# An attention-heavy two-block fp32 model on one core: the order of work around its attentions

## The reference, cut to what matters

```
# dilated mixer: 3 groups (window, dilation), 16 heads of 64, one softmax over the groups' shares
o = sum_g wts_g * softmax(q_g k_g^T / 8, masked) v_g ;  x = x + o @ w_o
# cross attention, per layer of the second block, 4 heads of 256
q = rmsnorm(x) @ wq ; k = rmsnorm(mem) @ wk ; v = rmsnorm(mem) @ wv
p = softmax(q k^T / 16) ; x = x + concat_h(p v) @ wo
```

## Time and profile before

| what | value |
|---|---|
| median of 3 runs | 1811.06 us (1810.83 to 1812.44) |
| the profiled execution: its time | 1810.18 us |
| its span | 1808.3 us |
| TensorE busy | 1749.3 us (97%) |
| VectorE, ScalarE, GpSimd busy | 1108.6, 896.3, 150.6 us |
| TensorE's granted clock, mean | 0.992 of full |
| DMA | 311.08 MB, mean 172 GB/s |

### The profile page before, as it was taken

The page is one execution under the profiler, slowest core; times in us unless marked ns, Lnnn a source line. Parts: engine busy times, 40 slices in busy tenths (PEclk is TensorE's granted clock), DMA queues, the critical chain, the costliest instruction groups (busy, mean ns, idle before and its releaser), DMA issues.

```text
span 1808.3 us, 22946 instructions
## 1 busy us (share of the span) xinstructions
PE 1749.3 (97%) x9397; PEld 1481.9 (82%) x9397; DVE 1108.6 (61%) x1299; ACT 896.3 (50%) x1049; POOL 150.6 (8%) x106
## 2 busy tenths in 40 slices
PE   8989999999989989999999999999999999999997
PEld 6787999878867778999988878788888887788886
DVE  7867655587666754655555775465555667455554
ACT  6554544465545544544456445544445544654442
POOL 1100000011262141000012000000003000000000
PEclk9989999999999999999999999999999999999999
DMA  8426555545524525455565456265555456446551
GB/s 290 163 96 208 184 187 187 186 146 187 180 70 142 172 84 188 168 202 188 187 208 165 161 216 203 80 200 186 186 186 188 148 204 214 140 128 209 186 186 70
DMA packets 160632, 311.08 MB, mean 172 GB/s; under 512 B 5691, under 2 KB 53312, under 8 KB 159760
## 3 DMA queue, kind: packets, MB, share of 16 engines
q1 hardware_dynamic: 158512, 299.33, 49.8%
q0 software_dynamic: 2016, 10.29, 1.5%
HBM read 304.35 MB, written 5.24 MB: 171 GB/s over the span
## 4 chain that ended last, share of the span: by engine, by line
PE 85%; DVE 8%; ACT 4%; issue 2%; DMA 1%; SPq 0%; DVEq 0%; ACTq 0%
PE ps L453 22%; PE ps L455 22%; PE ps L454 22%; PE ps L673 4%; PE ps L674 4%; PE ps L672 4%; PE ps L416 4%; DVE wlo L1419 3%; ACT whi L945 2%; DVE work L1567 1%; PE ps L909 1%; ACT work L1042 1%; PE ps L884 1%; DMA raw<-in_a_w_qkv 1%; DVE hT_lo L1446 0%
## 5 line engine op out<-in xcount | busy, mean ns | idle before, releaser
L1419 DVE TENSOR_TENSOR wlo<-raw,whi 128x2048 fp32r<-128x2048 f32 x279 | 642.6, 2307 | 448.5 <-ACT whi L945 448.4
L453 PE MATMUL ps<-whi,hT_hi 128*128 128x512 f32 x1936 | 762.0, 394 | 7.2 <-DVE hT_lo L1446 2.5
L455 PE MATMUL ps<-whi,hT_lo 128*128 128x512 f32 x1936 | 751.5, 388 | 0.0
L454 PE MATMUL ps<-wlo,hT_hi 128*128 128x512 f32 x1936 | 750.4, 388 | 0.0
L945 ACT ACTIVATE whi<-raw 128x2048 fp32r<-128x2048 f32 x279 | 533.7, 1914 | 376.4 <-PE ps L455 317.4
L453 PEld LDWEIGHTS ps<-whi,hT_hi 128*128 128x128 f32 x1936 | 363.8, 188 | 85.6 <-issue 10.3
L455 PEld LDWEIGHTS ps<-whi,hT_lo 128*128 128x128 f32 x1936 | 363.5, 188 | 76.1
L454 PEld LDWEIGHTS ps<-wlo,hT_hi 128*128 128x128 f32 x1936 | 364.0, 188 | 70.2
L672 PE MATMUL ps<-hT_hi,whi 128*128 128x256 f32 x640 | 183.5, 287 | 0.0
L673 PE MATMUL ps<-hT_lo,whi 128*128 128x256 f32 x640 | 182.2, 285 | 0.0
L674 PE MATMUL ps<-hT_hi,wlo 128*128 128x256 f32 x640 | 182.1, 285 | 0.0
(11 more groups left out here) (197 smaller groups left out, 1095.0 us busy)
## 6 DMA issues: line engine op xcount, KB each, us to landing
raw<-in_w_in SPq DMA_DIRECT2D x46, 1024.0 KB, 5.1
raw<-in_w SPq DMA_DIRECT2D x88, 512.0 KB, 4.5
raw<-in_m_w_up SPq DMA_DIRECT2D x32, 1024.0 KB, 5.3
raw<-in_m_w_down SPq DMA_DIRECT2D x32, 1024.0 KB, 4.8
raw<-in_kv_w SPq DMA_DIRECT2D x24, 1024.0 KB, 5.2
raw<-in_w SPq DMA_DIRECT2D x22, 1024.0 KB, 4.8
raw<-in_b_w_q SPq DMA_DIRECT2D x12, 1024.0 KB, 5.1
raw<-in_a_w_qkv SPq DMA_DIRECT2D x11, 1024.0 KB, 6.6
```

Of the source, the lines that this page charges most:

```text
L453: pe.matmul(acc, xh, wh, start=start and k == 0, stop=False)
L454: pe.matmul(acc, xh, wl, start=False, stop=False)
L455: ins = pe.matmul(acc, xl, wh, start=False, stop=stop and k == kc - 1)
L1419: vec.tensor_tensor(wlo[:, m % SPLIT, :], raw[:, m % RAW, :], whi[:, m % SPLIT, :], ALU.subtract).then_inc(*mark("lo_ready", ("lo", m)))
```

## The change

1. **Layer A, slot 11.** VectorE makes the memory's low parts at the start of the slot, ahead of the shares, the split and the maxima.
2. **Layer B.** TensorE does a hook's value products ahead of its scores. In the first half ScalarE copies both units of the probabilities, and VectorE none. In the second half VectorE makes the value products' low part ahead of the maxima.
3. **Cross attention.** Heads 0 and 1 are worked inside the second chunk of `xa_q`, heads 2 and 3 inside `xa_o`, whose tiles now come in the order (k 0 to 3, both column halves), (k 4 to 7, both column halves), the second column half in the SC banks. Probabilities have two buffers. GpSimd scales them by the reciprocals before they are transposed. The value products are made transposed, one bank per head, so that ScalarE (`xo_hi`) and VectorE (`xo_lo`) split them straight into `hT[1]`; the transposes of `nat` are gone. VectorE waits for GpSimd (`xshare`) before its splits.

```
-            for nm in ("w_o_2", "xa_q_2", "xa_o_2"):
+            for nm in ("w_o_2", "xa_q_2"):
                 for c in (0, 512): chunk_tiles(a[nm][l], c)
+            halves_tiles(a["xa_o_2"][l])
...
-        px = pnf[:, 4096:4608].rearrange("p (t c) -> p t c", t=T)
-        pxT = pnf[:, 4608:5120].rearrange("p (m c) -> p m c", m=2)
+        px = [b.rearrange("p (t c) -> p t c", t=T) for b in (pnf[:, 4096:4608], knf[:, 512:1024])]
+        pxT = [pnf[:, 4608 + 512 * j:5120 + 512 * j].rearrange("p (m c) -> p m c", m=2) for j in range(2)]
...
@@ -623,10 +624,10 @@
             def b_hook(hook):
 
                 half, step, p, turned = b_steps(hook)
+                if p is not None:
+                    b_av(half, p)
                 if step is not None:
                     b_scores(half, step)
-                if p is not None:
-                    b_av(half, p)
                 if turned is not None:
                     b_turn_p(half, turned)
                 if hook in B_TURNS:
...
@@ -868,49 +869,73 @@
                 chunk(hT[1], tm[0], early=lambda: merged_half(1))
                 chunk(hT[1], late=lambda: x_half(v + 1, 0))
 
-                chunk(hT[0], tx[v + 1], early=lambda: x_half(v + 1, 1))
-                chunk(hT[0])
-                uqx = c.tu
-                turn(qn, KD, lambda g: [("qn", l, g // 2, t) for t in range(T)])
+                uq_, up_ = [None] * 4, [None] * 4
+
+                def xa_turn_q(n):
+                    for g in range(2):
+                        uq_[2 * n + g] = c.tu + g
+                    turned_at["xq", l, n] = c.tu
+                    turn(qn[:, :, n * 512:(n + 1) * 512], 4, lambda g: [("qn", l, n, t) for t in range(T)])
 
                 def xa_scores(h):
-                    pe.wait_ge(*at("T free", uqx + h))
+                    pe.wait_ge(*at("T free", uq_[h]))
                     if h >= 2:
                         pe.wait_ge(*at("xexp", l, h - 2))
                     elif h == 0:
                         pe.wait_ge(*at("merged", l, T - 1, 1))
+                        pe.wait_ge(*at("mem back", l))
...
-                def xo_half(n):
-                    turn(nat[:, :, n * 512:(n + 1) * 512], 4, lambda g: [("xo", l, 2 * n + g, t) for t in range(T)])
-
-                pe.wait_ge(*at("mem back", l))
-                xa_scores(0)
+                def xa_turn_p(h):
+                    pe.wait_ge(*at("xshare", l, h))
+                    up_[h] = turned_at["xp", l, h] = c.tu
+                    transposes([px[h % 2][:, t, k * P:(k + 1) * P] for k in range(2) for t in range(T)])
+
+                def xa_values(h):
+                    pe.wait_ge(*at("T free", up_[h]))
+                    if h >= 2:
+                        pe.wait_ge(*at("xo lo", l, h - 2))
+                    for j in range(2):
+                        for k in range(2):
+                            d = h * 256 + j * P
+                            ins = pe.matmul(ps[:, OB + h % 2, j * S:(j + 1) * S], vm[:, k, d:d + P], pxT[h % 2][:, k, :],
+                                            start=k == 0, stop=k == 1)
+                    ins.then_inc(*mark("weighted", ("xav", l, h)))
+
+                def xa_middle():
+                    xa_values(0)
+                    xa_turn_p(1)
+
+                chunk(hT[0], tx[v + 1], early=lambda: x_half(v + 1, 1))
+                ch = c.ch
+                free = lambda t, half: ("acc free", ch - 1, t)
+                tile(hT[0], 0, ACCB, True, False, None, free, lambda: xa_scores(0), lambda: xa_turn_q(0))
                 xa_scores(1)
-                for h in range(4):
+                tile(hT[0], 4, ACCB, False, True, None, None, xa_middle, lambda: xa_turn_p(0))
+                c.ch += 1
+                xa_values(1)
+                xa_turn_q(1)
+                xa_scores(2)
+                xa_scores(3)
+                ch = c.ch
+                for h in range(2):
+                    pe.wait_ge(*at("xo lo", l, h))
+                tile(hT[1], 0, ACCB, True, False, None, lambda t, half: ("acc free", ch - 1, t), lambda: xa_turn_p(2))
+                xa_turn_p(3)
+                xa_values(2)
+                for h in (2, 3):
                     pe.wait_ge(*at("xexp", l, h))
...
+                tile(hT[1], 0, SCB, True, False, None, None, None, lambda: xa_values(3))
+                for h in (2, 3):
+                    pe.wait_ge(*at("xo lo", l, h))
+                tile(hT[1], 4, ACCB, False, True)
+                c.ch += 1
+                tile(hT[1], 4, SCB, False, True, None, None, None, lambda: x_half(v + 2, 0))
+                turned_at["xa end", l], turned_at["xa chunks", l], turned_at["xa tile", l] = c.tu, c.ch, c.m - 1
 
                 chunk(hT[0], tx[v + 2], early=lambda: x_half(v + 2, 1))
                 tu = []
...
@@ -1060,7 +1085,8 @@
                     b_out(half, p)
                 if turned is not None:
                     c.tu = turned_at["b p", half, turned]
-                    plain(b_pT[turned % 2][:, 0, :])
+                    for h in range(1 if half else 2):
+                        plain(b_pT[turned % 2][:, h, :])
                 if step is not None:
                     b_exps(half, step)
                 if hook in B_TURNS:
...
+                def xq_turn(n):
+                    c.tu = turned_at["xq", l, n]
+                    for g in (2 * n, 2 * n + 1):
+                        plain(qT[:, 2 * g:2 * g + 2, :].rearrange("p k s -> p (k s)"))
+
                 def xexps(h):
                     act.wait_ge(*at("xnegmax", l, h))
-                    if h:
-                        act.wait_ge(*at("T", uh[0]))
+                    if h >= 2:
+                        act.wait_ge(*at("T", turned_at["xp", l, h - 2]))
                     for t in range(T):
-                        ins = sc.activation(px[:, t, :], ps[:, SC + h % 2, t * S:(t + 1) * S], ACT.Exp, scale=256 ** -0.5,
+                        ins = sc.activation(px[h % 2][:, t, :], ps[:, SC + h % 2, t * S:(t + 1) * S], ACT.Exp, scale=256 ** -0.5,
                                             bias=mx[:, 4 + t:5 + t] if h % 2 else mx[:, 2 + t:3 + t],
                                             accum_out=st[:, 8 + 2 * h + t:9 + 2 * h + t])
                     ins.then_inc(*mark("exps", ("xexp", l, h)))
+                def xp_turn(h):
+                    c.tu = turned_at["xp", l, h]
+                    if h >= 2:
+                        act.wait_ge(*at("xav", l, h - 2))
+                    plain(pxT[h % 2].rearrange("p m c -> p (m c)"))
+
+                def xo_hi(h):
+                    act.wait_ge(*at("xav", l, h))
+                    sc.activation(hT[1][0][:, 2 * h:2 * h + 2, :].rearrange("p k s -> p (k s)"), ps[:, OB + h % 2, :], CP).then_inc(
+                        *mark("o_hi", ("xo hi", l, h)))
+
+                begin(v + 1, junk2)
+                tick()
+                out_of_acc(CP, lambda tt: qn[:, tt, 0:512], rs_of(v + 1))
+                tick()
+                xq_turn(0)
                 xexps(0)
...
+                tick()
+                xexps(1)
+                xp_turn(0)
+                xo_hi(0)
+                xp_turn(1)
+                out_of_acc(CP, lambda tt: qn[:, tt, 512:1024], rs_of(v + 1))
+                xo_hi(1)
+                xq_turn(1)
+                tick()
+                xexps(2)
+                xexps(3)
+                xp_turn(2)
+                tick()
+                xp_turn(3)
+                xo_hi(2)
+                xo_hi(3)
+                tick()
+                tick()
+                c.ch += 1
+                c.tu = turned_at["xa end", l] - 2
+                x_half(v + 2, 0)
...
@@ -1576,14 +1622,14 @@
             def b_hook(hook):
 
                 half, step, p, turned = b_steps(hook)
-                if step is not None:
-                    b_maxes(half, step)
                 if p is not None and half:
                     u = turned_at["b o", half, p]
                     dve.wait_ge(*at("T hi", u))
                     vec.tensor_tensor(by_token(hT[1][1][:, 4 + p, :]), by_position(ps[:, TB + u % 2, 0:S]),
                                       by_token(hT[1][0][:, 4 + p, :]), ALU.subtract).then_inc(*mark("lo_turned", ("T free", u)))
-                if turned is not None:
+                if step is not None:
+                    b_maxes(half, step)
+                if turned is not None and half:
                     u = turned_at["b p", half, turned] + 1
                     dve.wait_ge(*at("T", u))
                     vec.tensor_copy(b_pT[turned % 2][:, 1, :], ps[:, TB + u % 2, :]).then_inc(*mark("turned_v", ("T free", u)))
...
@@ -1709,6 +1755,9 @@
             vec.tensor_scalar(lamt[:, 5:6], lamt[:, 4:5], -LAM_INIT, None, ALU.add).then_inc(*mark("lambda_steps", ("neg lambda",)))
 
             for n in range(A_OUT):
+                if n == A_UNITS - 1:
+                    c.tu = turned_at["mem"]
+                    turn(4, hT[0], lambda k: gcol("mem0", k))
...
```

(68 more changed lines are left out.)

42 lines of the change are left out of this document (removed).

## The result

The changed kernel takes **1793.54 us** (median of 4 runs, 1792.98 to 1795.79) against 1810.94 us (4 runs, 1810.40 to 1812.44): a ratio of 0.9906, with the interval 0.9894 to 0.9918. The forecast was 1798.0 us, with a range from 1791.5 to 1804.5. The profiled execution is the slowest of the four, 1795.79 us, so from profile to profile 14.4 us went, where the sum said 13.0; the medians are 17.4 us apart. Much of the 3 us between the two is the clock: the four executions, from the slowest, took 1795.79, 1793.93, 1793.14 and 1792.98 us at mean granted clocks of 0.991, 0.993, 0.994 and 0.995. One execution further down, of the cross attention alone, was a slow one (2318.2 us at a mean clock of 0.703) and is in no ratio; without it that kernel's median is 1801.67 us.

A forecast was written before the change was run, and what follows sets the result against it. TensorE, busy 97% of the span, was taken to bound the kernel. Gains 2.1 + 0.3 + 4.2 + 6.4 = 13.0 us take the profiled 1810.2 to 1797.2; 0.9 for the median gives 1798.0 us, range 1791.5 to 1804.5 (own range 1794.5 to 1801.5).

The forecast's parts named there:

- Slot 11, 2.1 us: Layer A: with low parts ahead of the shares, TensorE's unit starts at 94.55 instead of 96.68; bounds 0 and 4.8 us.
- First half, 0.3 us: Layer B's dilated attention: value products stop waiting for copies, but transposes then wait for ScalarE's read-out; 0.3 us gained.
- Rival 1: Dilated attention, first half: its waits go as well, 8 us more gained, 1790 us; chance 0.12.
- one sign of being wrong: First half of the dilated attention: L616 (L617 after the change) or its successors start without a wait.
- Second half, 4.2 us: Layer B's dilated attention: two waits for low parts shrink by 1.3 us each, and one clock fall of 1.6 us goes.
- Cross attention, 3.2 us per layer: TensorE's 22.2 us per layer, less 17.3 of remaining work and 1.7 of new costs; 6.4 us for two layers.
- some eight seams: Cross attention: new switches between tile products and fp32 matmuls, taken at 0.15 us each, 1.2 us per layer.
- Only head 2 has none: Cross attention: head 2 has no slack, since VectorE does the maxima of head 3 ahead of head 2's reciprocal.
- Rival 2: Cross attention gives little: seams at 0.3 us and late probabilities leave 1 us per layer, 1802.4 us; chance 0.19.
- Rival 3: Whole change: the edits hold each other, only slot 11 and a little are left, 1808 to 1811 us; chance 0.05.
- Rival 4: Cross attention: GpSimd's shares, slowed beside VectorE's splits, make the kernel slower, 1818 us at d = 5.6; chance 0.03.
- The forecast's formula: Cross attention: if a head's pair of GpSimd shares takes d us, TensorE's waits total 4d - 12.5 us per layer.

The follow-up runs named there:

- again: Second batch of runs of the unaltered changed kernel, beside its parts on one chip: 1793.24 us, ratio 0.9902; profiled execution 1793.44 us.
- the doubled shares: Changed kernel with GpSimd's pair of shares made twice per head in the cross attention, the second after the first: 1800.62 us, ratio 0.9947.
- the early read-out: Changed kernel with VectorE, not ScalarE, reading out value products of pairs 0 and 2 (layer B, first half): 1793.16 us; also with slot 11's shares earlier: 1792.19 us.

## Why the prediction was right or wrong

**The verdict** was right (faster by over 0.2%, given 0.91), and the time lies inside the range and 4.5 us below the forecast, just under the forecast's own range (1794.5). The profiled execution of "again" (1793.44) is 3.8 us below the forecast's 1797.2: 3.0 us are the cross attention's, 0.3 the first half's, and 0.5 were there before any edit. The rest of the 4.5 us is most of the 0.9 us added for the median.

**Slot 11, 2.1 us.** Right: 2.0 and 2.1 from the tile product ahead of the slot; alone it gave 2.2 by the medians. The low parts went first, the shares were late next and released TensorE after 4.74 us, as forecast (4.7). The experiment with the shares made earlier confirms the reading of what was late next.

**First half, 0.3 us.** Right in reason, and somewhat low in size: the seven profiled executions that have this half as changed gained 0.1 to 1.4 us, 0.8 in the mean. The spread goes with the clock. From 505 to 555 us it was 0.86 in two of them (0.1 and 0.3 us gained), 0.90 in three (0.6, 1.0 and 1.1) and 0.93 in two (1.3 and 1.4); in the kernel before it was 0.90. The waits moved to the transposes, near 4 us twice, released by ScalarE's read-out. Rival 1, all 8.6 us gained, did not come: with the copies or the read-out changed the same waits only move, and with TensorE's order undone they stay. By its letter one sign of being wrong came true, as the products (L617) start with no wait at 506.62; the same paragraph forecasts that, and what stands behind them did wait. That the chain through VectorE's rotation sets it fits all of them, but no kernel shortened the rotation, so this part of the reason was argued and not tried.

**Second half, 4.2 us.** Right in size: 4.2 us where the clock stayed up, 2.7 where it fell, and the waits of 1.45, 0.79 and 1.77 us are the forecast 1.3, 0.7 and 1.8. The reason was half right. The maxima stood in the way; that ScalarE's high part is ready sooner "since the value products go first" was not needed, as the kernel with the scores first shows. The sentence "After 2.64 us of idling the clock fell, after 1.97 us it did not" was written as if it told where falls come. It told of one execution, and the forecast's full clock in this half did not come in the profiled one: the clock fell after 1.77 us in the profiled execution and not in "again", which has the same waits.

**Cross attention, 3.2 us per layer.** This is the step that failed, by size: 4.65 us per layer in both layers and both executions, close to the upper bound of 4.9. The term mis-sized is "New are some eight seams between tile products and fp32 matmuls ... I take 0.15": they cost nothing (1.72 us with both seams, 1.73 without), 1.2 us more. The waits were put at 0.5 and were 0.30 us of idle time, 0.2 us more. 3.2 + 1.2 + 0.2 = 4.6. Counted from start to start, as the prediction counts, that wait costs nearer 0.46 (1127.94 to 1129.28 is 1.34 us, and eight transposes elsewhere are 0.88), so some 0.2 us of the 4.65 have no term. The count of gaps and transposes behind the 3.2 was right. "Only head 2 has none" was wrong as well: its shares were there 1.05 us early, and the doubled shares show the same 1.1 us. GpSimd's instructions took 0.92 us in the mean of their records instead of 0.74, which that slack took in.

**The rivals.** Rival 2, seams of 0.3 us, was the opposite of what came. Rival 3 falls by the sum of the parts. Rival 4 was priced by 2.79 us for each instruction beside a split, d = 5.6; without the waits for `xshare` the pair beside a split took 3.80 us, and in the changed kernel 1.8. The Trainium skill's page "SBUF — State Buffer", section "Who interferes with whom", has a VectorE instruction with two SBUF inputs and a GpSimd one that reads SBUF exclude each other for a whole instruction. The trace agrees, with 3.80 against 1.83 us: the pair ended 1.69 us behind the split's end. The forecast's formula held: a doubled pair takes 3.76 us (1114.10 to 1117.86), for which it gives 2.5 us of waits per layer, and the doubled shares had 2.7. Rival 1 would have come to 1790, just outside the stated range that was to take in most of it.

**From profile to median.** The sum was made for a profiled execution and 0.9 us added for the median. The profiled execution of the changed kernel was 2.3 us above its median, most of it the stretch at 677.4: "again" had the same waits there at full clock and 1.5 us more gain in that half, and 0.5 more in the first.

## What to carry to other kernels

When two pieces of work in one queue are both ready, put the one that another engine waits for first, and ask before that who stands behind each: here one exchange of two VectorE instructions gave 4.2 us (2.7 of waits, 1.5 of low clock), and the exchange on TensorE beside it nothing. Where a block has gaps between short groups, hang the groups into a stream of other products and count the gaps as gained whole; what then decides is the slack of the hand-overs, which was measured here by doubling one of them. A wait that seems set by a chain through a third engine can change its place with an edit beside it and hardly its total, as in the first half.

## What was not expected of the hardware

- **Seams between kinds of products.** A group of eight 128 x 256 fp32 matmuls between fp32r tile products cost 1.72 us, among other fp32 matmuls 1.73 us.
- **Falls of the clock differ between executions of the same work.** In the second half, with waits of 1.45, 0.79 and 1.77 us, it fell behind the last one in the profiled execution of the changed kernel and in the one with the early read-out, and stayed up in eight others. With the old waits it fell behind the first, of 2.63 to 2.79 us, in the kernel before, with slot 11 alone and with VectorE's order undone, but with the cross attention alone behind those of 1.96 and 1.77 us and not behind that of 2.63. Once it fell at 382 us, behind waits of 1.2 us. In the two kernels with the early read-out it stayed full behind a wait of 3.4 us (at 521 us). Around the idle times of more than 4 us it was low in every profiled execution. A fall costs about 1.5 us here. In most kernels the slower executions are those with the lower mean clock; with the cross attention alone they are not.
- **GpSimd beside VectorE.** A share of 128 x 256 takes 0.91 us alone; a pair that began just behind a split took 3.80 instead of 1.83 us, and that split kept its 2.29 us. A split that began in the midst of shares took 2.51.
